# Window attention with scores two units ahead, three pairs of score buffers, and the division of the weights on GpSimd

## The reference

```python
s_band = jnp.einsum('bnqgrd,bnkgd->bngrqk', qb, kband).astype(jnp.float32) * scale
s_band = jnp.where(valid[None, :, None, None], s_band, NEG_INF)
s_meta = jnp.einsum('bnqgrd,bmgd->bngrqm', qb, meta_k).astype(jnp.float32) * scale
...
p = jax.nn.softmax(jnp.concatenate([s_sink, s_meta, s_band], axis=-1), axis=-1).astype(v.dtype)
o = (jnp.einsum('bngrqm,bmgd->bnqgrd', p[..., 1:1 + N_META], meta_v)
     + jnp.einsum('bngrqk,bnkgd->bnqgrd', p[..., 1 + N_META:], vband))
```

## Time and profile before

| | us |
|---|---|
| median of 3 runs (lowest, highest) | 3761.84 (3760.85, 3763.43) |
| profiled execution | 3763.35 |
| its span | 3761.4 |
| PE busy | 3624.0 (96%) |
| DVE busy | 1891.5 (50%) |
| ACT busy | 1361.8 (36%) |
| POOL busy | 471.0 (13%) |

### The profile page before, as it was taken

How to read it: one execution, slowest core, us unless ns; L and a number is a source line. 1 busy time by engine, 2 the same in 40 slices (tenths; PEclk the granted TensorE clock), 3 DMA queues, 4 the chain that set the end, 5 groups by cost and what they waited for, 6 DMA issues and landing times. The chain is left out here.

```text
span 3761.4 us, 58468 instructions
## 1 busy us (share of the span) xinstructions
PE 3624.0 (96%) x24178; PEld 3187.0 (85%) x24178; DVE 1891.5 (50%) x3307; ACT 1361.8 (36%) x2629; POOL 471.0 (13%) x571
## 2 busy tenths in 40 slices
PE   7999999999999999999999999999998999999998
PEld 6877778888888887888899889999997976888887
DVE  4544556555535546544455663443436556344444
ACT  3444444122224444322422452342233226244232
POOL 1222211000012333000111100110013110011001
PEclk9999999999999999999999999999999999999999
DMA  5111122333322112233311113222221111323332
GB/s 191 63 58 62 65 76 79 118 129 118 118 83 71 61 51 68 84 95 96 116 51 46 46 54 96 82 85 88 90 83 50 46 57 40 98 93 88 96 94 76
DMA packets 88247, 306.71 MB, mean 82 GB/s; under 512 B 10016, under 2 KB 13216, under 8 KB 87728
## 3 DMA queue, kind: packets, MB, share of 16 engines
q1 hardware_dynamic: 85184, 293.25, 24.2%
q0 software_dynamic: 2800, 9.73, 0.8%
HBM read 300.84 MB, written 2.10 MB: 81 GB/s over the span
## 5 line engine op out<-in xcount | busy, mean ns | idle before, releaser
L1920 DVE TENSOR_TENSOR weight_lo<-weight_raw,weight_hi 128x1024 fp32r<-128x1024 f32 (+1 forms) x464 | 560.9, 1212 | 427.9 <-ACT weight_hi L1322 427.5
L1322 ACT ACTIVATE weight_hi<-weight_raw 128x1024 fp32r<-128x1024 f32 (+1 forms) x464 | 476.7, 1031 | 576.7 <-PE bank L610 358.6
L610 PE MATMUL bank<-h_hi,weight_hi 128*128 128x512 f32 (+1 forms) x1328 | 481.6, 363 | 13.2 <-DVE h_lo L2356 9.1
L610 PE MATMUL bank<-h_hi,weight_lo 128*128 128x512 f32 (+1 forms) x1328 | 465.4, 350 | 0.0
L610 PE MATMUL bank<-h_lo,weight_hi 128*128 128x512 f32 (+1 forms) x1328 | 465.3, 350 | 0.0
L610 PE MATMUL bank<-u_hi,weight_hi 128*128 128x272 f32 (+2 forms) x1408 | 437.5, 311 | 3.2 <-DVE weight_lo L1920 3.2
L610 PE MATMUL bank<-u_lo,weight_hi 128*128 128x272 f32 (+2 forms) x1408 | 427.7, 304 | 0.0
L610 PE MATMUL bank<-u_hi,weight_lo 128*128 128x272 f32 (+2 forms) x1408 | 426.4, 303 | 0.0
L2779 POOL TENSOR_TENSOR scratch<-scratch 128x256 f32<-128x256 f32 (+2 forms) x132 | 113.8, 866 | 2019.3 <-ACT scratch L1360 2015.1
L610 PEld LDWEIGHTS bank<-h_hi,weight_hi 128*128 128x128 f32 x1328 | 253.2, 191 | 66.6 <-issue 29.9
L610 PEld LDWEIGHTS bank<-u_hi,weight_hi 128*128 128x128 f32 x1408 | 267.0, 190 | 30.4 <-issue 16.9
(11 more groups left out here) (320 smaller groups left out, 7914.8 us busy)
## 6 DMA issues: line engine op xcount, KB each, us to landing
weight_raw<-in_w_mlp SPq DMA_DIRECT2D x128, 512.0 KB, 3.5
weight_raw<-in_w_ff SPq DMA_DIRECT2D x128, 512.0 KB, 3.5
weight_raw<-in_w_in SPq DMA_DIRECT2D x92, 512.0 KB, 3.6
weight_raw<-in_w_mod SPq DMA_DIRECT2D x80, 512.0 KB, 4.4
weight_raw<-in_a_w_qkv SPq DMA_DIRECT2D x24, 512.0 KB, 3.8
weight_raw<-in_b_w_qkv SPq DMA_DIRECT2D x24, 512.0 KB, 3.6
first_weight<-in_w_mod SPq DMA_DIRECT2D x16, 512.0 KB, 15.2
weight_raw<-in_w_ret_o SPq DMA_DIRECT2D x16, 512.0 KB, 3.6
```

What stands on the lines that cost most here:

```text
L610: m = e.matmul(view[:, 0:hi - lo], a[:, k, :], b[:, k0 + k, lo:hi], start=(k == 0 and i == 0), stop=(k == kt - 1 and i == 2))
L1322: e.activation(whi[s % N_SPLIT][:, 0:kt, :], raw[n % N_RAW][:, 0:kt, :], ACT.Copy).then_inc(*tick("act_split", ("hi", n)))
L1920: e.tensor_tensor(wlo[s][:, 0:kt, :], raw[n % N_RAW][:, 0:kt, :], whi[s][:, 0:kt, :].bitcast(F32), ALU.subtract).then_inc(*tick("dve_split ...
```

## The change

`sweep_ahead` takes the place of `sweep` for the window attention alone. It starts with score(0), score(1), expo(0), norm(0) and a fill. Then for unit i: score(i+2), expo(i+1), turn_weights(i), norm(i+1), fill, turn_out(i-1), values(i). There is one fill a unit where there were two, and each hands out twice as much; the share of `Fill` is set to match.

The division is split in two, a stage `norm`: DVE takes the reciprocal, and POOL multiplies the weights by it. The score buffers are three pairs rather than two (`WS[i % 3]`), `w_small` has three slots of 16 columns rather than two of 32, and the waits for a buffer go back three units instead of two. `WWT` moves behind the third pair. Number and shapes of the instructions stay the same but for the engine of the division and ACT's table loads.

```diff
@@ -210,6 +210,30 @@
         if not joined or i + 1 == n:
             fill()
     return lambda: scale_out(n - 1), lambda: turn_out(n - 1)
+
+
+def sweep_ahead(n, stages, fill):
+
+    score, expo, turn_weights, norm, values, turn_out = stages
+    score(0)
+    score(1)
+    expo(0)
+    norm(0)
+    fill()
+    for i in range(n):
+        if i + 2 < n:
+            score(i + 2)
+        if i + 1 < n:
+            expo(i + 1)
+        turn_weights(i)
+        if i + 1 < n:
+            norm(i + 1)
+        fill()
+        if i > 0:
+            turn_out(i - 1)
+        values(i)
+    fill()
+    turn_out(n - 1)
 
 
 def beside(main, side, every):
...
@@ -399,8 +423,8 @@
                                            for i in range(3))
         near_meta = near_meta[0:N_META]
         W_S = SCR[:, :, :].rearrange("p a b -> p (a b)")
-        WS = [[W_S[:, 416 * (2 * i + s):416 * (2 * i + s) + 416] for s in range(2)] for i in range(2)]
-        WWT = [W_S[:, 1664 + 512 * s:1664 + 512 * s + 512] for s in range(2)]
+        WS = [[W_S[:, 416 * (2 * i + s):416 * (2 * i + s) + 416] for s in range(2)] for i in range(3)]
+        WWT = [W_S[:, 2496 + 512 * s:2496 + 512 * s + 512] for s in range(2)]
 
         def tab(j):
             return TAB[:, N_HYB * j:N_HYB * (j + 1)]
...
@@ -1207,7 +1231,7 @@
                         m = e.transpose(view[:, P * i:P * i + P], OA[:, 3, lo:lo + P], ident)
                     m.then_inc(*tick("pe_turn", job))
                     close(*job)
-                fill = Fill(2 * len(units) + 2, 7 * product_cost(wide(layer)) + 3.0, win_project(1, 2, 3),
+                fill = Fill(len(units) + 2, 7 * product_cost(wide(layer)) + 3.0, win_project(1, 2, 3),
                             *(gate_retention(m_) for m_ in range(4, KT)))
 
                 def score(i):
...
@@ -1256,8 +1280,7 @@
                     m.then_inc(*tick("pe_value", ("o", 2, layer, i)))
                     close("o", 2, layer, i)
 
-                for stage in sweep(len(units), (score, nothing, turn_weights, values, nothing, nothing), fill, joined=True):
-                    stage()
+                sweep_ahead(len(units), (score, nothing, turn_weights, nothing, values, nothing), fill)
                 fill.rest()
                 note("pe", "fence", "mix", layer, "pe")
                 for m_ in range(KT):
...
@@ -1801,8 +1824,7 @@
                     e.activation(OA[:, pr, q0:q0 + nq], view_of("o", 2, layer, i)[:, 0:nq], ACT.Copy).then_inc(
                         *tick("act_attn", ("free", "o", 2, layer, i)))
 
-                for stage in sweep(len(units), (score, expo, turn_weights, nothing, turn_out, nothing), fill, joined=True):
-                    stage()
+                sweep_ahead(len(units), (score, expo, turn_weights, nothing, nothing, turn_out), fill)
                 fill.rest()
                 flush(behind)
                 fence("mix", layer)
...
@@ -2642,10 +2664,10 @@
                     nb, root = P * len(ts), RI[0:nq, row_of(q0):row_of(q0) + 1]
                     for s in range(2):
                         job = ("s", 2, layer, i, s)
-                        view, x = view_of(*job), WS[i % 2][s][0:nq]
+                        view, x = view_of(*job), WS[i % 3][s][0:nq]
                         e.wait_ge(*at(*job))
-                        if i > 1:
-                            e.wait_ge(*at("t", 2, layer, i - 2, s))
+                        if i > 2:
+                            e.wait_ge(*at("t", 2, layer, i - 3, s))
                         e.tensor_scalar(x[:, 1:1 + N_META], view[0:nq, 0:N_META], root, None, ALU.mult)
                         e.scalar_tensor_tensor(out=x[:, 17:17 + nb], in0=view[0:nq, N_META:N_META + nb], scalar=root,
                                                in1=mask, op0=ALU.mult, op1=ALU.add).then_inc(
...
@@ -2653,24 +2675,18 @@
                     for s in range(2):
                         e.wait_ge(*at("sc", 2, layer, i, s))
                         e.wait_ge(*at("sink", layer, i, s))
-                        e.tensor_reduce(w_small(i, s, nq), WS[i % 2][s][0:nq, 0:17 + nb], AX, ALU.max,
+                        e.tensor_reduce(w_small(i, s, nq), WS[i % 3][s][0:nq, 0:17 + nb], AX, ALU.max,
                                         negate=True).then_inc(*tick("dve_attn", ("max", 2, layer, i, s)))
 
-                def expo(i):
-
-                    _, nq, ts, _ = geometry(units[i][1])
+                def norm(i):
+
+                    nq = geometry(units[i][1])[1]
                     for s in range(2):
                         e.wait_ge(*at("w", 2, layer, i, s))
                     e.reciprocal(w_small(i, 4, nq, 2), w_small(i, 2, nq, 2)).then_inc(
                         *tick("dve_attn", ("rc", 2, layer, i)))
-                    e.wait_ge(*at("rc", 2, layer, i))
-                    for s in range(2):
-                        x = WS[i % 2][s][0:nq, 1:17 + P * len(ts)]
-                        e.tensor_scalar(x, x, w_small(i, 4 + s, nq), None, ALU.mult).then_inc(
-                            *tick("dve_attn", ("n", 2, layer, i, s)))
-
-                for stage in sweep(len(units), (score, expo, nothing, nothing, nothing, nothing), fill, joined=True):
-                    stage()
+
+                sweep_ahead(len(units), (score, nothing, nothing, norm, nothing, nothing), fill)
                 fill.rest()
                 flush(behind)
                 fence("mix", layer)
...
@@ -3016,13 +3032,20 @@
                         fill(0.1)
                     nq = geometry(qi)[1]
                     for s in range(2):
-                        if i > 1:
-                            e.wait_ge(*at("w", 2, layer, i - 2, s))
-                        e.tensor_copy(WS[i % 2][s][0:nq, 0:1], vec("sink", 8 * layer + pr + 4 * s)[0:nq]).then_inc(
+                        if i > 2:
+                            e.wait_ge(*at("w", 2, layer, i - 3, s))
+                        e.tensor_copy(WS[i % 3][s][0:nq, 0:1], vec("sink", 8 * layer + pr + 4 * s)[0:nq]).then_inc(
                             *tick("pool_attn", ("sink", layer, i, s)))
 
-                for stage in sweep(len(units), (score, nothing, nothing, nothing, nothing, nothing), fill, joined=True):
-                    stage()
+                def norm(i):
+                    _, nq, ts, _ = geometry(units[i][1])
+                    e.wait_ge(*at("rc", 2, layer, i))
+                    for s in range(2):
+                        x = WS[i % 3][s][0:nq, 1:17 + P * len(ts)]
+                        e.tensor_scalar(x, x, w_small(i, 4 + s, nq), None, ALU.mult).then_inc(
+                            *tick("pool_attn", ("n", 2, layer, i, s)))
+
+                sweep_ahead(len(units), (score, nothing, nothing, norm, nothing, nothing), fill)
                 fill.rest()
                 fence("mix", layer)
                 for m_ in range(KT - TURN):
```

12 lines of the change are left out of this document (6 added, 6 removed).

## The result

The changed kernel takes 3772.18 us (median of 13 executions, 3767.92 to 3774.45), the kernel before beside it 3763.95 (13, 3760.85 to 3765.88): ratio 1.0022, 95% interval [1.0014, 1.0029]. It is slower by 8.2 us, where I had forecast it to be 5.8 us faster, at 3756.0, and called anything above 3764 unlikely. In the profiled executions the span went from 3761.4 to 3769.4 us.

A forecast was written before the change was run, and what follows sets the result against it. PE, busy 96% of the span, was taken as the bound, so only its idle time counts. Layer 0 -3.1, layer 1 +0.5, switches -1.5, end -0.85, clock -0.85: total -5.8 us, giving 3756.0; range 3747 to 3764.

The forecast's parts named there:

- Part 2: Regular units: POOL's division at 0.55 or 0.45 us is ready before PE's transposes need it, so no wait.
- Part 6: PE's order in both stretches: fewer switches from scores into projection matmuls, 30 x 0.05 = 1.5 us gained.
- Part 4: Rotations of q wait for ACT's copy: losses of 3.8 us plus 0.25 for S(4) in layer 1, 1.3 in layer 0.
- Part 5: Products with v wait behind ACT's exponentials: 1.1 us lost before V(16) in layer 0, 0.8 before V(13) in layer 1.
- Part 1: Stalls behind the sigmoids: transposes no longer wait there; all old stalls struck, 7.5 + 5.4 = 12.9 us gained.
- Part 3: First unit: its transposes T(0) wait for the division behind two scorings; 1.7 us lost in layer 0, 1.0 in layer 1.
- Part 7: End of layer 1: PE's stall 1.25 us rather than 2.1, gain 0.85; half the following clock drop's cost gone, 0.85.
- (C): Rival: POOL's division becomes the bound once a pair costs over 2.2 or about 2.5 us; 41 us, 3797; chance 0.07.

The follow-up runs named there:

- stand-in: Changed kernel with POOL's division replaced by a POOL copy of the same rows onto themselves, weights left undivided: 3759.08 us, ratio 0.9986 to the kernel before.
- one head each: Changed kernel with the division of a unit's first head on DVE and of its second head on POOL: 3762.67 us, ratio 0.9995 to the kernel before.

## Why the prediction was wrong, step by step

**Part 2 failed, by one price.** I put POOL's division at 0.55 and 0.45 us, from the copy row; it takes 1.28 and 0.96. I had two rows for POOL, a copy and an arithmetic operation, and took the one nearer in number of inputs, not the one nearer in kind. The bound stood in the text, and I left it there. The add's 0.71 for 256 elements, scaled, would have given 1.1 for 400. The division that part 2 followed behind a meta unit has 272 elements, 0.96 us, so its own chain is 0.1 + 2.38 + 0.17 + 0.1 + 0.96 = 3.7 where PE comes at 3.35. T(5) should then wait some 0.35, and it waited 0.27; T(10), the next such unit, waited 1.08, with a split beside its pair. T(7) shows a second way, which part 2 did not have. POOL's product for a rotation stood behind a pair of 2.54 us, DVE stood 1.96 us for that product and then did a split. So it began the scoring of unit 8 at 2150.44, 1.6 us after PE had finished those scores, and the reciprocal of unit 7 came behind that; T(7) waited 0.88.

The stand-in shows that this price is nearly all of the miss. With a copy of the price I assumed, the stretches were 98.6 and 91.7 us. My own terms, with six matmuls fewer in each stretch (counted afterwards; 0.12 and 0.23 us apiece) and the switches of part 6 halved between them, give 103.1 - 3.1 - 0.75 - 0.7 = 98.6 and 93.1 + 0.5 - 0.75 - 1.4 = 91.5. That they fit so closely is partly luck, since terms that were off cancelled each other (parts 4 and 5 below). Of the 16.2 us by which the forecast missed, 13.1 are changed kernel less stand-in, and 2.2 that the median of before was 3761.84 in three executions and 3764.0 later; 0.9 is left.

One slip of the working changes little: 4.9 us idle and four stalls of 0.16 make 5.5 us in layer 1, not 5.4.

The estimate from the Trainium skill ("GPSIMD Engine Reference", section 3.1), 0.6 us for 400 elements before dispatch, is less than half of what was measured, and its rate agrees with no row of this operation here: 633, 956 and 1284 ns for 144, 272 and 400 elements are some 0.25 us and 2.57 ns an element. For the 272 elements of a first unit that page's rate gives an estimate of 0.41 us, no more than my 0.45, so the 0.2 to 0.3 us more that I put on each first unit by it do not come out of it.

**How 0.7 us a division became 14.** Layer 0's stretch is 10.3 us longer than the stand-in's. 5.1 are the clock: the kernel with only q's copy moved has nearly the same waits of T there (0.3 us less), one drop rather than three, and a stretch 3.4 us shorter, so some 1.7 us a drop. The other 5.2 are waits, 4.5 of them idle time in the view. They are T(0), three more first heads, and second heads, since PE does a head's three or four transposes (0.52 or 0.63 us) in less time than POOL a division (0.96 or 1.28). Layer 1 is 4.0 us longer, by waits alone: no drop falls into it.

**Part 1 was right**: behind a sigmoid no first head of T waits any more (two second heads wait 0.4 and 0.3 us, for POOL), and with DVE dividing the new order gains 7 to 10 us, more than the 5.8 that I forecast. That is the order together with the third pair of buffers and the joined fills; they were not run apart.

**Part 3** was right with its price: the stand-in's T(0) stalls are 1.38 and 0.84 us idle, so 1.5 and 1.0 with the 0.16 that a stall costs besides, against 1.7 and 1.0. That a split shuts POOL out is in the rows (a pair of 1.91 took 2.80 beside 1.20 us of split). The Trainium skill ("SBUF — State Buffer", "Who interferes with whom") says so, and by that rule the trace agrees. A DVE multiplication with one SBUF input costs POOL too: with one head each, 1.52 us for 1.28 beside 0.43 us of it, and 1.13 for 0.96 beside 0.36. It goes the other way as well: with DVE dividing, a multiplication of 0.43 us took 1.52 at 3086.47 us, when it started together with POOL's product for a rotation. The same section of the Trainium skill names `tensor_scalar` among the operations that can contend so, and the trace agrees.

**Part 4**: three rotations in layer 1 at 3.7 us idle, 3.8 forecast; 1.4 in layer 0, 1.3 forecast. S(4) was 0.92, not 0.25, since POOL's product stood behind the pair.

**Part 5** was too dear by 1.2 us: V(16) waited 0.3, V(13) 0.4. S behind ACT's copies out, which I didn't list, waited 0.6 twice and made up for it.

**Part 6** can be judged only through the stretches' lengths, which it fits; no run shows it by itself.

**Part 7**: 1.37 us idle, some 1.5 from start to start, where I gave 1.25. The drop of the clock behind it is in none of the twelve executions profiled in the new order or a variant of it; I had counted half.

**The rivals.** The changed kernel lies between my forecast and (C), whose point of decision, a pair over 2.2 and 2.5 us, was about where it starts: a pair took 1.91 or 2.54. But I priced (C) only at its worst, 41 us, with nothing between, and gave all of it 0.07. Between the stand-in (0.52 us, 3759.1) and the changed kernel (1.28, 3772.2) a straight line gives 3769 for a division at the add's 1.1: the range should have reached there and past it, since the add's worst row was the upper bound, and it ended at 3764.

## What to carry to other kernels

Price an operation that the trace doesn't hold by the row nearest in kind on that engine: on GpSimd a multiplication took 2.5 times as long as a copy of the same size. Before moving work to a slower engine, ask where in the chain it stands: GpSimd's division cost 16.6 us of the stretches behind the scoring, against the same order with VectorE dividing, and 0.3 once its reciprocal stood ahead of the scoring. And follow everything else in that engine's queue, down to two copies of 0.15 us.
